# Four expert weight chunks of a two-block transformer kernel loaded ahead into free memory by GpSimd's queue

## What is computed

```python
def expert_choice_ffn(h, w_router, w1, w3, w2):
    n_tok, d = h.shape[1], h.shape[2]
    cap = EC_FACTOR * n_tok // N_EXPERTS
    aff = jax.nn.softmax(jnp.einsum('bnd,de->bne', h, w_router).astype(jnp.float32), axis=-1)
    gate, idx = lax.top_k(jnp.swapaxes(aff, 1, 2), cap)
    xs = jax.vmap(lambda hb, ib: hb[ib])(h, idx)
    a = jnp.einsum('becd,edf->becf', xs, w1)
    b = jnp.einsum('becd,edf->becf', xs, w3)
    y = jnp.einsum('becf,efd->becd', jax.nn.silu(a) * b, w2) * gate[..., None].astype(h.dtype)
```

## Time and profile before

| | |
|---|---|
| time of the runs, median (lowest to highest) | 2356.55 us (2355.02 to 2359.05), 3 runs |
| the profiled execution: its own time, and its span | 2353.34 us, 2351.6 us |
| PE busy; PEld busy | 2004.7 us (85%); 1494.5 us (64%) |
| DVE busy; ACT busy; POOL busy | 1002.1 us (43%); 748.9 us (32%); 7.1 us (0%) |
| moved by DMA | 643.78 MB, mean 274 GB/s |
| queue q1 (SP's), share of the 16 engines' span | 637.14 MB, 67.1% |
| queue q0 (POOL's) | 4.23 MB, 0.5% |

### The profile page before, as it was taken

The page is one execution under the profiler, slowest core; times in us unless marked ns, Lnnn a source line. Parts: engine busy times, 40 slices in busy tenths (PEclk is TensorE's granted clock), DMA queues, the critical chain, the costliest instruction groups (busy, mean ns, idle before and its releaser), DMA issues.

```text
span 2351.6 us, 37879 instructions
## 1 busy us (share of the span) xinstructions
PE 2004.7 (85%) x16424; PEld 1494.5 (64%) x16424; DVE 1002.1 (43%) x1908; ACT 748.9 (32%) x1338; POOL 7.1 (0%) x16
## 2 busy tenths in 40 slices
PE   5999898989897889756565656999999999998998
PEld 4777664444443757644343444878888877887887
DVE  3445522212121545401010103656567756556776
ACT  3344400000000625200000003655454446654544
POOL 0000000000000000000000000000000000000000
PEclk9999999999999999877887877999999999999999
DMA  9867279999999521599999996434445533345451
GB/s 398 313 251 304 92 316 427 428 427 427 427 427 427 231 92 37 222 427 425 427 426 426 426 426 258 177 130 157 179 179 195 199 143 144 144 179 188 180 199 69
DMA packets 45571, 643.78 MB, mean 274 GB/s; under 512 B 5168, under 2 KB 5440, under 8 KB 6496
## 3 DMA queue, kind: packets, MB, share of 16 engines
q1 hardware_dynamic: 44352, 637.14, 67.1%
q0 software_dynamic: 1056, 4.23, 0.5%
HBM read 640.30 MB, written 1.05 MB: 273 GB/s over the span
## 4 chain that ended last, share of the span: by engine, by line
PE 61%; DMA 32%; DVE 3%; ACT 2%; issue 1%; SPq 0%; ACTq 0%; DVEq 0%; POOLq 0%
PE bank L883 58%; DMA ring<-in_stream 31%; PE bank L891 3%; DMA arena<-in_b_masks 0%; DVE weights_low L2443 0%; DVE tokens_low L2008 0%; ACT arena L1835 0%; ACT ring L1710 0%; DVE arena L2543 0%; DVE ring L2246 0%; DVE arena L2119 0%; ACT weights_high L1547 0%; ACT arena L1579 0%; DVE x L2059 0%; DVE arena L2173 0%
## 5 line engine op out<-in xcount | busy, mean ns | idle before, releaser
L883 PE MATMUL bank<-ring,arena 128*32 128x128 f32 (+4 forms) x7928 | 638.0, 381 | 225.8 <-DMA ring<-in_stream 221.8
L883 PEld LDWEIGHTS bank<-ring,arena 128*32 128x32 f32 (+1 forms) x7928 | 375.6, 135 | 458.5 <-DMA ring<-in_stream 283.0
L2443 DVE TENSOR_TENSOR weights_low<-ring,weights_high 128x1024 fp32r<-128x1024 f32 (+2 forms) x288 | 343.5, 1195 | 274.2 <-ACT weights_high L1547 269.0
L1547 ACT ACTIVATE weights_high<-ring 128x1024 fp32r<-128x1024 f32 (+2 forms) x288 | 297.8, 1035 | 285.5 <-PE bank L883 285.0
L883 PE MATMUL bank<-weights_high,tokens_high_low 128*128 128x512 f32 (+2 forms) x1152 | 359.3, 386 | 12.0 <-DVE tokens_high_low L2455 10.1
L883 PEld LDWEIGHTS bank<-weights_high,tokens_high_low 128*128 128x128 f32 x1152 | 215.3, 190 | 57.3 <-DVE tokens_high_low L2455 10.7
L1547 ACT ACTIVATE arena<-bank 128x256 f32<-128x256 f32 (+6 forms) x254 | 104.4, 435 | 393.1 <-PE bank L891 306.8
L883 PE MATMUL bank<-weights_low,tokens_high_low 128*128 128x512 f32 (+2 forms) x576 | 219.2, 381 | 0.0
L2163 DVE TENSOR_TENSOR arena<-arena,bank 128x256 f32<-128x256 f32 (+1 forms) x64 | 22.7, 354 | 453.4 <-PE bank L883 453.4
L1671 ACT ACTIVATE arena<-bank 128x256 f32<-128x256 f32 (+1 forms) x64 | 21.1, 330 | 590.5 <-PE bank L883 590.5
L2173 DVE TENSOR_TENSOR arena<-bank,arena 32x512 f32<-32x512 f32 (+1 forms) x128 | 70.8, 553 | 269.6 <-PE bank L883 268.3
(11 more groups left out here) (206 smaller groups left out, 2095.3 us busy)
## 6 DMA issues: line engine op xcount, KB each, us to landing
ring<-in_stream SPq DMA_DIRECT2D x302, 2048.0 KB, 22.7
x<-in_x_in SPq DMA_DIRECT2D x1, 2048.0 KB, 10.3
arena<-in_od_pack POOLq DMA_DIRECT2D x1, 1024.0 KB, 12.8
arena<-in_gains POOLq DMA_DIRECT2D x2, 512.0 KB, 5.9
out<-arena SPq DMA_DIRECT2D x1, 1024.0 KB, 4.0
arena<-in_b_masks POOLq DMA_DIRECT2D x1, 896.0 KB, 11.3
arena<-in_ev_pack POOLq DMA_DIRECT2D x1, 582.0 KB, 12.0
ring<-in_ev_pack POOLq DMA_DIRECT2D x1, 512.0 KB, 10.7
```

Source lines behind the costliest of these rows:

```text
L883: ins = pe.matmul(o, lhsT, rhs, start=start, stop=stop)
L1547: ins = act.activation(o, i, ACT.Copy)
L2443: dve.tensor_tensor(dst, whole, high.bitcast(F32), ALU.subtract).then_inc(sig, 1)
```

## The change

Four expert chunks leave the ring: chunk 6 of `moe0`, and chunks 6, 7 and 8 of `moe1`. SP skips them in the stream. POOL loads each in two halves of 1 MB into regions of `arena` (one half of one chunk into the context half of `x`), behind waits for the last users of these regions, and PE reads them from there behind a semaphore of their own. To make room, the projection `mix1` gets its own buffers, sized for its two token tiles, the router's result and the final gain move to other offsets, and the normed tokens of layer 1 take a smaller region. The other chunks keep their order; the slot each of them gets shifts by one place in the cycle after `moe0` chunk 6, and by three more after `moe1` chunk 8.

```diff
+EXTRA = (("moe0", 6), ("moe1", 6), ("moe1", 7), ("moe1", 8))
 RING_SLOTS = (3, 1, 4, 5, 0, 2)
...
     for key in in_ring + [("mix1", c) for c in range(2)] + [("moe1", k) for k in range(6 * N_EXP)]:
-        put(key, next(ring))
+        put(key, None if key in EXTRA else next(ring))
...
+MIX1_WEIGHTS = ((19456, 19968), (20480, 20992), (4096, 4608))
+CAT1_HI, CAT1_LO, MIX1_TMP = 0, 17408, 5120
+EXTRA_AT = ((9216, 15360), (None, 13312), (9216, 2048), (6144, 15360))
...
-MOE_XN, MOE_HT, MOE_YST, MOE_OH, MOE_AFF = 0, 4096, 4096, 8192, 10240
+MOE_XN, MOE_HT, MOE_YST, MOE_OH, MOE_AFF = 0, 4096, 4096, 8192, 22528
...
-FINAL_G = (15360, 1024)
+FINAL_G = (18432, 1024)
...
+        def extra_halves(n):
+
+            return [region(at, CHUNK // 2) if at is not None else X[:, TT:2 * TT, :].rearrange("p a b -> p (a b)") for at in EXTRA_AT[n]]
+
+        def moe_rows(moe, at, k, rows):
+
+            if (moe, at) in EXTRA:
+                half = extra_halves(EXTRA.index((moe, at)))[2 * k // rows]
+                return half.rearrange("p (k n) -> p k n", k=rows // 2)[:, k % (rows // 2)]
+            return chunk(moe, at).rearrange("p (k n) -> p k n", k=rows)[:, k]
...
                 s = slot_of(n)
+                if s is None:
+                    continue
                 if loads_of(n) > 1:
                     sp.wait_ge(slot_free[s], freed_for(n))
...
+            def load_extra(n, half):
+                at, size = CHUNK_AT[EXTRA[n]], CHUNK // 2
+                load(extra_halves(n)[half], stream[at][:, half * size:(half + 1) * size], f"extra_in{n}")
+
+            Banks(pool).drained("sgu", 3)
+            load_extra(0, 0)
+            pool.wait_ge(sem("z_used"), Z_USED_UP_TO[Z_AT["mix0", 1, 3]])
+            load_extra(0, 1)
+
             x_done(pool, 0, 2 * TT - 1)
             load(region(OD_SHIFT, 4 * P + 3 * 512), od_pack, "od_in")
             load(region(OD_ROPE, 4 * 16), od_rope, "od_in2")
+
+            Banks(pool).filled("odatt", ("o", len(OD_UNITS) - 1))
+            for n in (2, 3):
+                for half in range(2):
+                    load_extra(n, half)
+            load_extra(1, 0)
+            Banks(pool).filled("cat1", KD - 1)
+            load_extra(1, 1)
 
             pool.wait_ge(sem("x_mix"), 12)
             load(final_g[0], gains[0], "fg_in")
...
+                def chunk_in(at):
+                    if (moe, at) in EXTRA:
+                        pe.wait_ge(sem(f"extra_in{EXTRA.index((moe, at))}"), 32)
+                    else:
+                        arrived(moe, at)
+
+                def chunk_done(at):
+                    if (moe, at) not in EXTRA:
+                        used(moe, at)
```

More of the change, by code:

```diff
@@ L714, in program @@
         od_cat = region(OD_CAT, TT, D)
-        moe_ht = region(MOE_HT, KD, 512)
+        moe_ht = [region(MOE_HT, KD, 512), region(MOE_HT, KD, SEQ)]
         moe_xn = region(MOE_XN, 4, D)
@@ L733, in program @@
         moe_yst = region(MOE_YST, 2, D)
-        mix_tmp = region(MIX_TMP, 2, 512)
+        mix_tmp = [region(at, 2, 512) for at in (MIX_TMP, MIX1_TMP)]
         spare_ring = ring[:, len(B2_SLOTS):SLOTS, :].rearrange("p a b -> p (a b)")
@@ L798, in program @@
         z_weights = {name: [[parts(f"{name}_{part}{n}", at, 512) for part, at in zip(("high", "low"), ats)] for n, ats in enumerate(places)]
-                     for name, places in (("evz", EV_WEIGHTS), ("odz", OD_WEIGHTS), ("mix", MIX_WEIGHTS))}
-        z_weights["mix0"] = z_weights["mix1"] = z_weights["mix"]
+                     for name, places in (("evz", EV_WEIGHTS), ("odz", OD_WEIGHTS), ("mix0", MIX_WEIGHTS), ("mix1", MIX1_WEIGHTS))}
+        c1_hi, c1_lo = parts("mixed1_high", CAT1_HI, KD, SEQ), parts("mixed1_low", CAT1_LO, KD, SEQ)
+        def extra_halves(n):
[5 more added lines that the diff above has]
+            return chunk(moe, at).rearrange("p (k n) -> p k n", k=rows)[:, k]
         in_ring = ring_at + 4 * (SPARE_SLOTS[0] * CHUNK + SPARE_W)
@@ L937, in z_product @@
                 _, wh, wl = z_piece(name, c, k)
+                high, low = (c1_hi, c1_lo) if name == "mix1" else (z_hi, z_lo)
                 for t in range(tiles):
@@ L941, in z_product @@
                     cols = slice(t * P, (t + 1) * P)
-                    for q, (x, w) in enumerate(((z_hi, wh), (z_hi, wl), (z_lo, wh))):
+                    for q, (x, w) in enumerate(((high, wh), (high, wl), (low, wh))):
                         sig = None
@@ L1078, in combine @@
                            moe_yst[:, t // TT, c * 512:(c + 1) * 512], True, True, fills("comb" + L, (g, n)))
+                def chunk_in(at):
[6 more added lines that the diff above has]
+                        used(moe, at)
                 def hidden(g, e, key, c):
                     at = (g * PER_GROUP + e) * 6 + c
-                    arrived(moe, at)
+                    chunk_in(at)
                     b.vacant(moe, (g, e, key))
                     xs = moe_x(streams)[:, :, e].rearrange("p k s c -> p k (s c)")
-                    w = chunk(moe, at).rearrange("p (k n) -> p k n", k=KD)
                     o = bank(moe, (g, e, key))
@@ L1092, in hidden @@
                             last = k == KD - 1 and q == parts - 1
-                            mm(o[q * rows:(q + 1) * rows, 0:width], xs[:, k, :], w[:, k, q * width:(q + 1) * width],
+                            mm(o[q * rows:(q + 1) * rows, 0:width], xs[:, k, :], moe_rows(moe, at, k, KD)[:, q * width:(q + 1) * width],
                                k == 0, k == KD - 1, fills(moe, (g, e, key)) if last else None)
-                    used(moe, at)
+                    chunk_done(at)
                 def turn_hidden(g, e, c):
@@ L1104, in down @@
                 def down(g, e, c, kts):
-                    w = chunk(moe, (g * PER_GROUP + e) * 6 + 4 + c).rearrange("p (k n) -> p k n", k=4)
+                    at = (g * PER_GROUP + e) * 6 + 4 + c
                     o = bank(moe, (g, e, "y"))
@@ L1111, in down @@
                             last = c == 1 and kt == 3 and n == parts - 1
-                            mm(o[n * rows:(n + 1) * rows, 0:yw], lhs, w[:, kt, n * yw:(n + 1) * yw],
+                            mm(o[n * rows:(n + 1) * rows, 0:yw], lhs, moe_rows(moe, at, kt, 4)[:, n * yw:(n + 1) * yw],
                                c == 0 and kt == 0, c == 1 and kt == 3, fills(moe, (g, e, "y")) if last else None)
@@ L1136, in experts @@
                         down(g, e, 0, (2, 3))
-                        used(moe, at)
-                        arrived(moe, at + 1)
+                        chunk_done(at)
+                        chunk_in(at + 1)
                         b.drained(moe, (g, e, "t1"))
                         down(g, e, 1, (0, 1, 2, 3))
-                        used(moe, at + 1)
+                        chunk_done(at + 1)
                 settle()
@@ L1632, in cat_split @@
                     b.filled("cat1", k)
-                    copy(z_hi[:, k, 0:width], bank("cat1", k)[:, 0:width], sem("cat_hi"))
+                    copy(c1_hi[:, k, :], bank("cat1", k)[:, 0:width], sem("cat_hi"))
                     if k == 1:
@@ L1748, in _ @@
             b.drained("modcol0", 1)
-            norm_out("n2_0", moe_ht, 4, A2[0], B2[0])
+            norm_out("n2_0", moe_ht[0], 4, A2[0], B2[0])
             experts(0)
@@ L1820, in _ @@
             square_sums(X, moe_xn, TT, lambda t: act.wait_ge(sem("x_mix"), 8 + TT + t + 1))
-            norm_out("n2_1", moe_ht, TT, A2[1], B2[1])
+            norm_out("n2_1", moe_ht[1], TT, A2[1], B2[1])
             experts(1)
@@ L2066, in mix_add @@
                 cols = slice(c * 512, (c + 1) * 512)
-                add_gated(name, (c, t), bc[:, t // TT, cols], X[:, t, cols], mix_tmp[:, t % 2], 512, sem("x_mix"))
+                tmp = mix_tmp[name == "mix1"]
+                add_gated(name, (c, t), bc[:, t // TT, cols], X[:, t, cols], tmp[:, t % 2], 512, sem("x_mix"))
             def cat_low(layer, k, whole, width, sig):
+                high, low = (c1_hi, c1_lo) if layer else (z_hi, z_lo)
                 dve.wait_ge(sem("cat_hi"), KD * layer + k + 1)
-                dve.tensor_tensor(z_lo[:, k, 0:width], whole, z_hi[:, k, 0:width].bitcast(F32), ALU.subtract).then_inc(sig, 1)
+                dve.tensor_tensor(low[:, k, 0:width], whole, high[:, k, 0:width].bitcast(F32), ALU.subtract).then_inc(sig, 1)
             def mix1():
@@ L2332, in _ @@
             scaled(X, moe_xn, 4, 8)
-            norm_out("n2_0", 4, moe_ht, A2[0], B2[0])
+            norm_out("n2_0", 4, moe_ht[0], A2[0], B2[0])
             experts(0)
@@ L2414, in _ @@
             scaled(X, moe_xn, TT, 14)
-            norm_out("n2_1", TT, moe_ht, A2[1], B2[1])
+            norm_out("n2_1", TT, moe_ht[1], A2[1], B2[1])
             experts(1)
```

2 lines of the change are left out of this document (1 added, 1 removed).

## The result

The changed kernel took 2332.39 us in the median (2330.28 to 2334.52, 4 runs) against 2355.78 us (2352.81 to 2359.05, 4 runs). The ratio is 0.9904, interval 0.9891 to 0.9916. The forecast was 2336.8 us, from 2333 to 2342.5, 19.7 us less. Repeated on three later occasions, each beside new runs of the kernel before, the ratio was 0.9918, 0.9914 and 0.9914, that is 19 to 20 us. The first median lies 0.6 us under the range; of the repetitions 2336.15 and 2336.43 us lie in it and 2332.45 us just under it. The profiled execution took 2334.52 us, with a span of 2332.7 us, 18.9 us less than before.

A forecast was written before the change was run, and what follows sets the result against it. Both expert stages were taken to be bound by unbroken DMA up to their last landing. Savings of 4.9 us (stage 0) and 14.8 us (stage 1), 19.7 us in all, took the median from 2356.55 to 2336.8 us, range 2333 to 2342.5.

The forecast's parts named there:

- What bounds the two stages: Both expert stages end when their last chunk lands; each chunk loaded ahead saves one DMA time, 4.9 and 14.8 us.
- rival 1: Only one part pays: PE cannot use stage 0's chunk, or stage 1's POOL loads land slowly; 2341.8 us, chance 0.08.
- formula for the last landing: Stage 0: last landing is when PE is done with chunk 0 (307.67 us) plus (96 - 6) chunks at DMA's rate.
- The new loads land in time: Stage 1: six POOL loads of 1 MB land before PE wants chunk 6, at 987 us at the earliest.
- quick end: Stage 1: 7.8 us for each 1 MB POOL load, 47 us for six, all there at 972 us.
- The slow end: Stage 1: six POOL loads one after another, 77 us, the last at 1002 us; DMA would idle 0 to 5 us.
- The size of PE's waits in stage 1: PE's waits for the ring in stage 1 fall from 168.7 to about 154 us.
- The time between the stages: Stage 0's last landing to PE's first chunk of stage 1: growth beyond 220.6 us would make the prediction wrong.
- The other two signs: Prediction wrong if DMA's share drops under 1 within a stage, or if PE waits for one of the new loads.
- The mixer was not slowed: Projections ahead of the stages: 6 MB landing beside them cost nothing; DVE's split takes 688 ns or 694 ns.
- the second stack begins as before: Behind stage 1: `b_masks` holds the chain for 11.30 us and its load moves along unchanged.
- allowance of 2 us: From 925 to 978 us: if PE's low-clock stretch grows or shrinks by 4 us, the time moves by 2.

## Why the prediction was right

- **What bounds the two stages** was right. One DMA time for each chunk: stage 0 became 5.0 us shorter for 4.9 forecast, and stage 1 14.6 us for 14.8. Eight profiles have stage 0's chunk loaded ahead (442.6 to 442.8 us, for 447.6 to 447.8), nine have stage 1's (439.3 to 439.6 us from PE's first expert product to the last landing, for 454.0 to 454.2). PE could cash in stage 0's chunk (rival 1): the chain goes over to DMA at 362 us, forecast 358. The prediction's formula for the last landing is short by a fixed part, since 307.67 + 90 x 4.91 = 749.6 us and the landing was at 755.4; it drops out of the difference, which is all that the sum uses.
- **The new loads land in time**: at 9.7 and 13.7 us each, overlapping, in place of 7.8 one after another. The prediction's quick end had the six done 47 us after the first issue. From 923 to 936 us DMA moved 426 GB/s, and the slowest of the six took 15.6 us to land, so all were there by 938 us, 18 us after the first issue. The slow end (12.8 us each, strictly in a row) did not come either. Its cost of up to 5 us doesn't follow from its own working, which gives 1014 - 1012 = 2 us; nothing came to hang on it.
- **The size of PE's waits in stage 1** was forecast at 154 us and came out at 160.6. The prediction took the whole 14.8 us out of the waits. But PE's busy time in the stage fell too, from 273.5 to 262.9 us (granted clock 0.80 and 0.82), and its idle time with nothing to wait for ("issue") rose from 3.2 to 7.1 us: -8.1 - 10.6 + 3.9 = -14.8 us. It has no bearing on the end, which the last landing sets.
- **The time between the stages** nearly kept its length: from stage 0's last landing to PE's first expert product of stage 1 it took 970.75 - 749.67 = 221.1 us, 220.6 before. Read to the letter this is one of the prediction's signs of being wrong, by 0.5 us; the three repetitions took 220.6, 220.9 and 220.9 us, so it is scatter. The other two signs did not show: DMA's share stayed at 1.01 in both stages, and PE waited for none of the new loads.
- **The mixer was not slowed** by the landing data (busy times from 920 to 973 us, above). **The new layout and the queue** make no difference beyond the scatter of their experiments.
- **What was overlooked**: the prediction said the second stack begins as before, and looked only at `b_masks`. For four chunks it does so but for 0.9 us (922.3 to 922.5 us behind the last landing in four profiles, 921.4 before; the cause is open), and only because of where four chunks leave the rotation. With three of them 8 us would have gone, as the experiment with stage 1's chunks alone shows.
- **The surplus of the first measurement** was scatter, which arises ahead of stage 0. In two profiles of the same changed kernel, taken with the second and the third repetition, SP's first load behind chunk 0 goes out at 304.38 and at 309.89 us, and the spans are 2329.9 and 2335.4 us: the 5.5 us between the spans are there before the first expert chunk is done. The first 300 us of the two (columns as above), first the quicker one:

```profile
0.00:300.00 300.00, 254.01 (x2782) 206.43 (x2783) 144.39 (x406) 119.28 (x265) 4.48 (x12) 0.97 0.70 273
```

```profile
0.00:300.00 300.00, 256.00 (x2734) 206.17 (x2734) 140.09 (x394) 119.28 (x265) 4.48 (x12) 0.95 0.70 273
```

In the same 300 us the quicker one shows 48 matmul records more, at a granted clock of 0.97 for 0.95. That goes the right way; that the clock alone makes the 5.5 us was not tried. Over all 13 profiles, variants included, that first load goes out between 301.6 and 310.0 us. The prediction's allowance of 2 us was for the clock from 925 to 978 us; for the start of the kernel it had none. That this scatter put the first median under 2333 us fits, but isn't shown: only one of its executions has a trace.

## What to carry to other kernels

- Where a stage streams more than fits into memory, each buffer filled before the stage begins is worth one transfer time, as long as the transfer engines never idle inside the stage and PE still waits for landings. That held here with PE busy 387 of 440 us and 273 of 443 us alike. Look for the idle stretch ahead of it and for memory that is dead in just that stretch. Which queue issued the loads made no difference here.
- The same buffers filled while the stage runs made it slower: the chunks that PE wants next share DMA with later ones, PE waits for them, and the ring fills and stands.
- Taking a buffer out of a ring turns the ring. Look at which slot the last chunk of the stage ends in, and which slot the first load of the next stage wants.

## What was not expected of the hardware

The start of the kernel, up to the first load behind chunk 0, took 304.4 us in one execution and 309.9 in another of the same kernel, with the granted clock over its first 300 us at 0.97 and 0.95; all that followed took 2025.5 us in both. And the six loads of 1 MB, issued within 3 us, took as long to land from the software queue (9.7 us in the median) as from SP's (9.5 us), with DVE busy 32.4 of 53 us beside them. By the rule of the Trainium skill, "SBUF — State Buffer", section "Who interferes with whom", DVE in a two-port mode would hold up POOL's descriptors. These runs show no such delay, but they don't test the rule: the same section says that `tensor_tensor` has no two-port mode, and from 920.9 to 938 us, when the six had landed, everything that DVE did in the changed kernel was TENSOR_TENSOR. So the prediction's up to 5 us by that rule had no ground at this place, whatever DVE's busy share.
